# LayerNorm seams of a two-block transformer kernel, by token halves; even_in's banks read by ScalarE

## The chip, the cores and the metric

One core of one Trainium2 chip runs the whole program. The metric is the device time of one execution in microseconds (us). The kernel before took 2296.6 us, the median of three runs (2296.34 to 2301.74).

## The reference

The input is x of 512 tokens by 1024 channels in float32. Two blocks follow one another. The first has a qkv projection, banded attention, an RWKV mixer, gates, an output product and a squared-ReLU feed-forward, with RMS norms. The second has two layers; each is a mixer, a LayerNorm, a convolutional feed-forward and a LayerNorm:

```python
for layer in range(2):
    y = even_mixer(x, ...) if layer % 2 == 0 else odd_mixer(x, ...)
    x = layer_norm(ALPHA * x + y, ln1_g[layer], ln1_b[layer])
    f = conv_ffn(x, ffn_w_up[layer], ffn_conv_w[layer], ffn_conv_b[layer], ffn_w_down[layer])
    x = layer_norm(ALPHA * x + f, ln2_g[layer], ln2_b[layer])

def layer_norm(x, g, b):
    mu = x.mean(-1, keepdims=True)
    var = jnp.square(x - mu).mean(-1, keepdims=True)
    return (x - mu) * lax.rsqrt(var + LN_EPS) * g + b
```

The mean runs over the 1024 channels of a token. Tokens are independent in it. Even_mixer's first product gives 28 tiles of 128 channels with a bias and, for some, a scale.

## The kernel before

**Layout.** Everything is held channel-major: x is 8 tiles (KD = 8) of 128 channels by 512 tokens, `x[:, t, :]`. A dense product computes one output tile (128 by 512, one PSUM bank) as a sum over k. Each k takes three matmuls of 512 columns: high weight part by high input part, high by low, low by high (L321 to L323 in `split_product`). Weights come as a stream of units of eight 128 by 128 blocks. SP loads a unit into one of 3 raw buffers. ACT writes its rounded high part (L169), POOL subtracts that for the low part (L178), into one of 3 split buffers. A split buffer comes free when the last matmul on its unit has run. The classes `Weights`, `Signal` and `Chain` keep the counts; the semaphores of one engine's wait are written out by hand.

**A seam.** Between a stage that ends in a residual and the stage that follows lies a LayerNorm over all channels. There are four: even_out (n_k = 4 blocks per tile) to ffn_up_0, ffn_down_0 (n_k = 22) to odd_in, odd_out (n_k = 8) to ffn_up_1, and ffn_down_1 (n_k = 22) to the last stage, which only norms and stores. `stage_linear` (L1975) computes eight tiles. DVE adds each bank to x (L2073), and to a running sum of x (L2082); ACT squares the tile (L2044) and DVE adds the square to a running sum (L2052). PE waits for no norm there, it only needs banks.

After the eighth tile `layer_norm` (L569) runs, all on 512 tokens. PE turns the three sums into columns of 4 numbers per partition by matmuls of one column (`column_sums`, L434). DVE makes mean and variance in `col` (L595 to L601, 128 by 4), ACT takes the root (L465), DVE the reciprocal (L460), and PE spreads mean and factor over partitions with 8 matmuls of 128 columns (`spread_columns`, L440). Then for each of 8 tiles: DVE adds the negative mean (L607) and scales (L612), in pairs; ACT writes the high part of x plus bias (L589) and x plus bias (L590); POOL subtracts for the low part (L498).

`first_products` (L327) takes the first three tiles of the next stage (AT_FIRST = 3) in step with that. For each of the first six k it waits for the high part, issues two matmuls for each of three tiles (L341, L342), waits for the low part, and issues one for each (L347). So a k gives PE nine matmuls of 512 columns. The last two k of each tile come at the end. All three units of these tiles must be split before.

**The weight queue at a seam.** `Weights.ahead` lets ACT and POOL prepare units up to two beyond those released. In front of the norm's work ACT has one `round_high` and POOL one `subtract_low`, so that three units are ready.

**even_in.** Sixteen jobs (`EVEN_FIRST`) write banks 0 to 3 in turn: twelve tiles and four transposes of tokens (`turn_token`, L937). PE waits before job n for the read of job n - 4. DVE reads each bank (L2196 and L2297), and between two reads does the gates' work for that job number (`gates_dve`, L2238): sums, a scan over tokens, and four calls of `split_rows` (L726, with L731, L732, L734) which writes rows in three bf16 parts. ACT here only rounds weight units and runs `gates_act` at job 5, two pairs of Exp and Ln.

**The last stage.** After each tile's L590, SP stores 256 KB of it to `out_t` (L3096), and waits for all eight.

Of the kernel before, what the change touches and what calls it, by code (L numbers as in the profile page):

```python
# [22 lines left out]
NT = T // P  # L23
D = 1024
# [159 lines left out]
class Before:  # L184

    def __init__(self, pe, act, dve, pool, high, ready, counts, order=tuple(range(KD))):
# [12 lines left out]
def network(nc, x_t, vectors, constants, rel_rev, stream, bias_line, bias_rows, gate_rows, out_t):  # L201
    n_units = stream.shape[0]
    ctx = ExitStack()
    with ctx:
# [93 lines left out]

        side_pe, side_act, side_dve = Signal(sem("side_pe")), Signal(sem("side_act")), Signal(sem("side_dve"))
# [67 lines left out]

        def product(pe, n_tiles, n_k, rhs, read, before=None, beside=None, prior=None, late=None):


            if before is not None:
                before.pe(pe)
                first_products(pe, rhs, before)
                if beside is not None:
                    beside(pe, 1)
# [9 lines left out]
        def weight_programs(block, act=True, before=None):  # L385
# [8 lines left out]
            def _(pool):  # L394
                if before is not None:
                    wts.subtract_low(pool, G, u0 + 1)
                    before.pool(pool)
# [171 lines left out]
        def layer_norm(name, layer, split=True):  # L569

            def pe(p):
                p.wait_ge(norm_dve.sem, norm_dve.at(-1))
                column_sums(p, SUMS, 4, (w[:, SQ_SUM, :],))
                p.wait_ge(norm_dve.sem, norm_dve.at(0))
                column_sums(p, MEAN, 4, (w[:, X_SUM, :],))
                p.wait_ge(norm_act.sem, norm_act.at(0))
                column_sums(p, FACTOR, 4, (w[:, LAST_SQ, :],))
                p.wait_ge(norm_dve.sem, norm_dve.at(1))
                spread_columns(p, SPREAD_MEAN, 0)
                p.wait_ge(norm_dve.sem, norm_dve.at(3))  # L580
                spread_columns(p, FACTOR, 8)

            def act(a):
                root_after_linear(a, LN_EPS, 2)
                for t in range(KD):
                    b = v(name + "_b", KD * layer + t)
                    a.wait_ge(norm_dve.sem, norm_dve.at(t + 4))
                    if split:
                        S.activation(xs[:, 0, t, :], xt(t), ACT.Identity, bias=b).then_inc(norm_high.sem, 1)  # L589
                    S.activation(xt(t), xt(t), ACT.Identity, bias=b).then_inc(norm_act.sem, 1)  # L590

            def dve(d):
                mean, var = col[:, 0:4], col[:, 4:8]
                d.wait_ge(norm_pe.sem, norm_pe.at(2))
                V.tensor_scalar(mean, bank(MEAN, 4, 4), -1.0 / D, None, ALU.mult).then_inc(norm_dve.sem, 1)  # L595
                d.wait_ge(norm_dve.sem, norm_dve.at(1))
                dve_chain.link(d, V.scalar_tensor_tensor(var, bank(MEAN, 4, 4), -1.0 / D, mean, ALU.mult, ALU.mult))
                dve_chain.link(d, V.scalar_tensor_tensor(var, bank(SUMS, 4, 4), 1.0 / D, var, ALU.mult, ALU.subtract))
                d.wait_ge(norm_pe.sem, norm_pe.at(3))
                dve_chain.link(d, V.scalar_tensor_tensor(var, bank(FACTOR, 4, 4), 1.0 / D, var, ALU.mult, ALU.add))  # L600
                V.tensor_scalar(var, var, 0.0, None, ALU.max).then_inc(norm_dve.sem, 1)  # L601
                factor_dve(d, 1)

                def centred(t):
                    if t == 0:
                        d.wait_ge(norm_pe.sem, norm_pe.at(4))
# [2658 lines left out]
```

## Time and profile before

| | |
|---|---|
| runs | 2296.34, 2296.6, 2301.74 us; median 2296.6 us |
| profiled execution | 2297.78 us, span of the profile 2296.0 us, so 1.8 us lie around it |
| PE busy | 2182.6 us, 95% of the span |
| DVE, ACT, POOL busy | 1008.6, 830.9 and 818.6 us |
| mean granted TensorE clock | 0.961 of full speed |

PE runs nearly through. What isn't PE on the chain that ended last is the seams, the chunks of the mixers, and a few waits for DVE. Matmuls of 512 columns last 0.39 us by their rows, and start 0.227 us apart, so a stretch of them is read by starts.

### The profile page before, as it was taken

The page shows a single profiled execution, that of the slowest core. Times are in us where ns is not written, and L with a number is a line of the kernel's source. Part 1 is how long each engine was busy: PE and PEld are TensorE (multiplying, and loading weights), DVE is VectorE, ACT ScalarE, POOL GpSimd, SP SyncE. Part 2 cuts the span into 40 slices and gives each one's busy share as a digit, 9 for nine tenths or more (in the row PEclk, how much of TensorE's full clock was granted, in tenths as well). Part 3 has the DMA queues.
Part 4 walks back from the last instruction along what each step waited for, and adds up shares of the span by engine and source line. Part 5 has one row for each costly group of instructions (what it writes and reads, how often), then busy time and mean ns, then how long its engine had stood idle before and what let it go on. Part 6 is the DMA issues. An engine that isn't in the chain of part 4 may idle for free.

```text
span 2296.0 us, 29683 instructions
## 1 busy us (share of the span) xinstructions
PE 2182.6 (95%) x12396; PEld 1754.9 (76%) x12404; DVE 1008.6 (44%) x1636; ACT 830.9 (36%) x1268; POOL 818.6 (36%) x362
## 2 busy tenths in 40 slices
PE   8999989999899999999997899999999889999997
PEld 6767788888778888776776688888877477888886
DVE  4222855436531121345337644442268465444323
ACT  4345511134342242232335344442243334444322
POOL 4423300034244444442231344444444024444442
PEclk9999988799999999999999899999999989999998
DMA  7222200014223233221111122232312012322331
GB/s 264 92 69 83 74 2 3 2 56 156 74 83 101 92 101 101 83 73 65 47 56 40 53 92 92 96 104 95 101 57 90 19 55 65 102 100 92 101 98 58
DMA packets 53005, 182.97 MB, mean 80 GB/s; under 512 B 5752, under 2 KB 5760, under 8 KB 52744
## 3 DMA queue, kind: packets, MB, share of 16 engines
q1 hardware_dynamic: 52872, 181.08, 23.6%
q8 instruction: 98, 1.61, 0.3%
q14 instruction: 35, 0.29, 0.0%
HBM read 176.32 MB, written 7.62 MB: 80 GB/s over the span
## 4 chain that ended last, share of the span: by engine, by line
PE 87%; DVE 9%; ACT 2%; issue 1%; POOL 1%; DMA 0%; DVEq 0%; SPq 0%; ACTq 0%
PE ps L321 19%; PE ps L323 19%; PE ps L322 19%; PE ps L1506 3%; PE ps L2500 2%; PE ps L341 1%; PE ps L2502 1%; PE ps L347 1%; PE ps L2501 1%; PE ps L342 1%; PE ps L1036 1%; PE ps L3036 1%; PE ps L434 1%; PE ps L1038 1%; PE ps L1037 1%
## 5 line engine op out<-in xcount | busy, mean ns | idle before, releaser
L178 POOL TENSOR_TENSOR split_units<-raw_units,split_units 128x1024 fp32r<-128x1024 f32 x314 | 760.2, 2429 | 1423.2 <-ACT split_units L169 1423.2
L321 PE MATMUL ps<-x_split,split_units 128*128 128x512 f32 x1224 | 482.8, 394 | 8.6 <-POOL split_units L178 6.3
L169 ACT ACTIVATE split_units<-raw_units 128x1024 fp32r<-128x1024 f32 x314 | 329.9, 1052 | 437.9 <-PE ps L323 380.1
L322 PE MATMUL ps<-x_split,split_units 128*128 128x512 f32 x1224 | 478.2, 391 | 0.0
L323 PE MATMUL ps<-x_split,split_units 128*128 128x512 f32 x1224 | 477.9, 390 | 0.0
L321 PEld LDWEIGHTS ps<-x_split,split_units 128*128 128x128 f32 x1224 | 230.9, 189 | 62.8 <-issue 6.5
L322 PEld LDWEIGHTS ps<-x_split,split_units 128*128 128x128 f32 x1224 | 230.9, 189 | 49.2 <-issue 1.7
L323 PEld LDWEIGHTS ps<-x_split,split_units 128*128 128x128 f32 x1224 | 230.9, 189 | 48.6
L321 PE MATMUL ps<-hidden_split,split_units 128*128 128x512 f32 x608 | 237.3, 390 | 0.0
L323 PE MATMUL ps<-hidden_split,split_units 128*128 128x512 f32 x608 | 236.6, 389 | 0.0
L322 PE MATMUL ps<-hidden_split,split_units 128*128 128x512 f32 x608 | 236.5, 389 | 0.0
L2831 DVE SCALAR_TENSOR_TENSOR work<-ps,vec,work 128x511 f32<-128x511 f32 x88 | 66.0, 750 | 225.3 <-ACT work L2820 224.9
L322 PEld LDWEIGHTS ps<-hidden_split,split_units 128*128 128x128 f32 x608 | 114.1, 188 | 24.1 <-issue 0.5
L321 PEld LDWEIGHTS ps<-hidden_split,split_units 128*128 128x128 f32 x608 | 114.1, 188 | 24.0 <-issue 0.5
L323 PEld LDWEIGHTS ps<-hidden_split,split_units 128*128 128x128 f32 x608 | 114.1, 188 | 23.9
L2820 ACT ACTIVATE work<-ps,vec 128x512 f32<-128x512 f32 x88 | 68.6, 780 | 168.0 <-PE ps L323 149.9
L2073 DVE TENSOR_TENSOR x<-x,ps 128x512 f32<-128x512 f32 x29 | 19.9, 687 | 142.0 <-PE ps L323 141.6
L2833 DVE SCALAR_TENSOR_TENSOR work<-ps,vec,work 128x510 f32<-128x510 f32 x88 | 65.9, 749 | 3.1
L2811 ACT ACTIVATE hidden_split<-work 128x512 fp32r<-128x512 f32 x44 | 27.8, 632 | 103.1 <-DVE work L2841 103.1
L1506 PE MATMUL ps<-work 64*64 64x64 f32 x1920 | 64.1, 232 | 0.0
L1506 PEld LDWEIGHTS ps<-work 64*64 64x64 f32 x1920 | 63.6, 148 | 0.1
L341 PE MATMUL ps<-x_split,split_units 128*128 128x512 f32 x120 | 50.8, 423 | 10.6 <-ACT x_split L589 5.0
(434 smaller groups left out, 3283.9 us busy)
## 6 DMA issues: line engine op xcount, KB each, us to landing
raw_units<-stream SPq DMA_DIRECT2D x314, 512.0 KB, 3.4
bias_rows<-bias_line SPq DMA_DIRECT2D x1, 2816.0 KB
gate_rows<-work SPq DMA_DIRECT2D x10, 256.0 KB, 2.1
work<-gate_rows SPq DMA_DIRECT2D x10, 256.0 KB, 2.7
x<-x_t SPq DMA_DIRECT2D x4, 512.0 KB, 6.5
work<-bias_rows SPq DMA_DIRECT2D x1, 2048.0 KB
out_t<-x SPq DMA_DIRECT2D x8, 256.0 KB
vec<-vectors SPq DMA_DIRECT2D x1, 1159.5 KB, 9.2
```

Of the source, the lines that this page charges most:

```text
L169: scalar.activation(self.split[:, u % SPLIT, 0, :], self.raw[:, u % RING, :], ACT.Copy).then_inc(self.high_done, 1)
L178: gpsimd.tensor_tensor(self.split[:, u % SPLIT, 1, :], self.raw[:, u % RING, :], self.split[:, u % SPLIT, 0, :].bitcast(F32), ALU.subtract ...
L321: TE.matmul(out, high, rhs(0, k), start=(k == 0), stop=False)
L322: TE.matmul(out, high, rhs(1, k), start=False, stop=False)
L323: ins = TE.matmul(out, low, rhs(0, k), start=False, stop=last and shift is None)
L341: TE.matmul(bank(m), high, rhs(0, k), start=(i == 0), stop=False)
L1506: ins = TE.matmul(ps[r, out, i * HD:(i + 1) * HD], left(i, r), right(i, r), start=True, stop=True)
L2500: TE.matmul(bank(b % 2), high, a[0], start=(k == 0), stop=False)
L2811: S.activation(hidden2[:, 0, j, :], w[:, y0 + 2 * j % 4, :], ACT.Copy).then_inc(high_out.sem, 1)
L2820: S.activation(w[:, y0 + m % 4, :], bank(m % 4), ACT.Identity, scale=taps(m)[2], bias=v("ffn_b", layer * 44 + (m % 2) * FF2 + m // 2)).the ...
L2831: dve_chain.link(dve, V.scalar_tensor_tensor(y[:, 1:T], b[:, 0:T - 1], taps(m)[1], y[:, 1:T], ALU.mult, ALU.add))
L2833: V.scalar_tensor_tensor(y[:, 2:T], b[:, 0:T - 2], taps(m)[0], y[:, 2:T], ALU.mult, ALU.add).then_inc(tile_read.sem, 1)
```

## The change

It does these things:
- `TH = 256`. The eighth tile of the stage in front of each LayerNorm is computed by `last_by_halves`: all k on tokens 0 to 255 into bank 3, then all k on tokens 256 to 511 into bank 2. In the middle of the first half PE turns the sum of seven squares into columns, at k = 4 of the second half (3 where n_k = 4) it does the column sums of the first 256 tokens, and where n_k = 22 it spreads their mean and factor at k = 13.
- The class `LayerNorm` takes the place of `layer_norm`. Every step exists once for each half. The orders on each engine are written out: DVE does the first three tiles of half 0, then the residual of half 1, two more tiles, the variance of half 1, two more, the reciprocal, the last, then half 1's eight.
- `first_halves` takes the place of `first_products` at these seams. It does tiles 0 and 1 on half 0 for each k, with the column sums of half 1 after k = 3; then the spread of half 1, tile 2 on half 0, and tiles 0, 1, 2 on half 1.
- ACT rounds the first unit of the next stage before the root, the second after it, the third behind tile 4 of half 0. POOL takes the third at tile 5. (In even_out two of them and in odd_out one are still rounded in the stage before.)
- The last stage stores 16 pieces of 128 KB instead of 8 of 256 KB.
- even_in's banks are read by ScalarE. The query scale of 1/8 moves into scale and a scaled bias. The two semaphores on which even_mix waited for DVE's row splits become `ready_out`.

The diff, cut to its core:

```diff
+        def first_halves(pe, rhs, seam):
...
+            def one_block(m, h, k):
+                if k == 0 and h == 0:
+                    pe.wait_ge(wts.low_done, unit + m + 1)
+                high, low = (wts.split[:, (unit + m) % SPLIT, part, k * P:(k + 1) * P] for part in range(2))
+                out = bank(m, h * TH, TH)
+                TE.matmul(out, high, rhs(0, k)[:, tokens(h)], start=(k == 0), stop=False)
+                TE.matmul(out, low, rhs(0, k)[:, tokens(h)], start=False, stop=False)
+                seam.ready(pe, h, k)
+                return TE.matmul(out, high, rhs(1, k)[:, tokens(h)], start=False, stop=(k == UNIT - 1))
+
+            for k in range(UNIT):
+                seam.high(pe, 0, k)
+                for m in range(2):
+                    one_block(m, 0, k)
+                if k == 3:
+                    seam.sums(pe, 1)
+            seam.spread(pe, 1)
+            pe.wait_ge(seam_dve.sem, seam_dve.at(seam.READ_B))
+            for k in range(UNIT):
+                one_block(2, 0, k)
+            for m in range(AT_FIRST):
+                for k in range(UNIT):
+                    seam.high(pe, 1, k)
+                    ins = one_block(m, 1, k)
...
+            def act(self, act):
...
+                wts.round_high(act, S, u0 + 1)
+                root(0)
+                wts.round_high(act, S, u0 + 2)
                 for t in range(KD):
...
+                    tile(0, t)
+                    if t == 2:
+                        self.square(act, 1)
+                    if t == 4:
+                        wts.round_high(act, S, u0 + 3)
+                        root(1)
+                for t in range(KD):
+                    tile(1, t)
...
+                variance(0)
+                factor(0)
+                tiles(0, 0, 3)
+                self.residual(dve, 1)
+                tiles(0, 3, 5)
+                variance(1)
+                tiles(0, 5, 7)
+                factor(1)
+                tiles(0, 7, KD)
+                tiles(1, 0, KD)
...
+                        if h == 0 and t == 5:
+                            wts.subtract_low(pool, G, self.unit + 3)
...
+            def last_by_halves(pe):
...
+                for h in range(2):
+                    b = bank(3 - h, h * TH, TH)
+                    for k in range(n_k):
...
+                        TE.matmul(b, high, src(0, k)[:, tokens(h)], start=(k == 0), stop=False)
+                        TE.matmul(b, high, src(1, k)[:, tokens(h)], start=False, stop=False)
+                        ins = TE.matmul(b, low, src(0, k)[:, tokens(h)], start=False, stop=last and not scaled)
...
+                        if h == 0 and k == n_k // 2:
+                            pe.wait_ge(norm_dve.sem, squares_added(KD - 2))
+                            seam.sums_before(pe)
+                        if h == 1 and k == min(4, n_k - 1):
+                            seam.sums(pe, 0)
+                        if h == 1 and k == 13:
+                            seam.spread(pe, 0)
...
+                def residual(dve, h):
+                    xh = x[:, KD - 1, tokens(h)]
+                    dve.wait_ge(tile_ready.sem, ready_at[h])
+                    V.tensor_tensor(xh, xh, bank(3 - h, h * TH, TH), ALU.add).then_inc(seam_dve.sem, 1)
+                    dve.wait_ge(seam_dve.sem, seam_dve.at(4 * h + seam.READ_A))
+                    V.tensor_tensor(w[:, X_SUM, tokens(h)], w[:, X_SUM, tokens(h)], xh, ALU.add
+                                    ).then_inc(seam_dve.sem, 1)
...
                     if n >= 4:
-                        pe.wait_ge(tile_read.sem, tile_read.at(n - 3))
+                        pe.wait_ge(read_act.sem, read_act.at(n - 3))
...
-                for n, (kind, m) in enumerate(EVEN_FIRST):
-                    dve.wait_ge(tile_ready.sem, tile_ready.at(n + 1))
-                    if kind == "tile":
-                        even_tile(m, n % 4).then_inc(tile_read.sem, 1)
-                    else:
-                        V.tensor_copy(w[:, 40 + m, :], bank(n % 4)).then_inc(tile_read.sem, 1)
+                for n in range(n_jobs):
                     gates_dve(dve, n)
...
                     wts.round_high(act, S, u0 + tiles + SPLIT)
                     gates_act(act, n)
+                    act.wait_ge(tile_ready.sem, tile_ready.at(n + 1))
+                    if kind == "turn":
+                        ins = S.activation(w[:, 40 + m, :], bank(n % 4), ACT.Copy)
...
+                        ins = S.activation(w[:, m, :], bank(n % 4), ACT.Identity, bias=v("ev_b", m))
+                    ins.then_inc(read_act.sem, 1)
```

## Rows read from the trace of the kernel before

**Rows 1.** The page, the chain that ended last, shares by engine.
```profile
PE 87%; DVE 9%; ACT 2%; issue 1%; POOL 1%; DMA 0%; DVEq 0%; SPq 0%; ACTq 0%
```

**Rows 2.** Waits of PE, 985 to 1092 us: us in total, times, longest us.
```profile
PE ps L937 <- DVE work L2297: 5.6, 1, 5.6
```

**Rows 3.** Timeline, end of even_in: start us, us, engine and line; PE, then DVE.
```profile
1032.93 0.66 PE L937 MATMUL ps<-con,work 128*128 128x128 f32 x4
1039.13 1.11 PE L937 MATMUL ps<-con,work 128*128 128x128 f32 x4 [5.55 <-DVE work L2297]
1041.33 0.63 PE L321 MATMUL ps<-x_split,split_units 128*128 128x512 f32 x1
...
1038.39 1.29 DVE L2297 COPY work<-ps 128x512 f32<-128x512 f32 x2
```

**Rows 4.** Windows of 4 us: length, busy PE, PEld, DVE, ACT, POOL, granted clock, DMA.
```profile
1036.00:1040.00 4.00, 0.86 (x5) 0.87 (x5) 3.81 (x9) 0.00 (x0) 0.00 (x0) 0.52 0.41 131
1040.00:1044.00 4.00, 4.00 (x14) 3.17 (x13) 3.66 (x9) 0.00 (x0) 0.00 (x0) 0.62 0.01 2
...
1907.00:1911.00 4.00, 2.08 (x8) 1.78 (x8) 2.70 (x6) 0.76 (x2) 0.00 (x0) 0.50 0.43 131
```

**Rows 5.** Seam behind ffn_down_0, timeline; its last row is the chain's.
```profile
1673.70 0.39 PE L323 MATMUL ps<-hidden_split,split_units 128*128 128x512 f32 x1
...
1682.42 0.72 ACT L589 ACTIVATE x_split<-x,vec 128x512 fp32r<-128x512 f32 x1 [3.15 <-DVE x L612]
...
1683.68 0.73 ACT L589 ACTIVATE x_split<-x,vec 128x512 fp32r<-128x512 f32 x1
1683.84 10.10 POOL L498 TENSOR_TENSOR x_split<-x,x_split 128x512 fp32r<-128x512 f32 x8 [4.93 <-ACT x L590]
...
1700.43 6.96 PE ps L2878 x16
```

**Rows 6.** Ends of the other three seams, timeline: PE, and ACT for the last.
```profile
1299.51 0.39 PE L2007 MATMUL ps<-first_high,mean_weights 128*128 128x512 f32 x1
...
1330.17 0.50 PE L321 MATMUL ps<-x_split,split_units 128*128 128x512 f32 x1 [1.55 <-POOL split_units L178]
...
1901.61 0.39 PE L323 MATMUL ps<-odd_split,split_units 128*128 128x512 f32 x1
...
1932.00 0.50 PE L321 MATMUL ps<-x_split,split_units 128*128 128x512 f32 x1 [1.56 <-POOL split_units L178]
...
2275.55 0.39 PE L323 MATMUL ps<-hidden_split,split_units 128*128 128x512 f32 x1
...
2292.14 1.38 ACT L590 ACTIVATE x<-x,vec 128x512 f32<-128x512 f32 x2 [0.54 <-DVE x L612]
```

**Rows 7.** Groups by line and shape: busy us, mean ns; the last row is timeline.
```profile
L612 DVE SCALAR_TENSOR_TENSOR x<-x,vec,ps 128x512 f32<-128x512 f32 x32 | 23.4, 742 | 2.8 <-PE ps L440 2.8
...
L1655 DVE TENSOR_TENSOR work<-ps,con 128x256 f32<-128x256 f32 x40 | 17.0, 425 | 9.3 <-PE ps L1506 7.9
...
L1118 ACT ACTIVATE work<-work,col 128x256 f32<-128x256 f32 x8 | 4.0, 502 | 2.5 <-DVE col L1069 2.5
...
L169 ACT ACTIVATE split_units<-raw_units 128x1024 fp32r<-128x1024 f32 x314 | 329.9, 1052 | 437.9 <-PE ps L323 380.1 <-PE ps L347 27.5 <-PE ps L792 9.2
...
L178 POOL TENSOR_TENSOR split_units<-raw_units,split_units 128x1024 fp32r<-128x1024 f32 x314 | 760.2, 2429 | 1423.2 <-ACT split_units L169 1423.2
...
1676.95 0.16 DVE L597 SCALAR_TENSOR_TENSOR col<-ps,col 128x4 f32<-128x4 f32 x1
```

**Rows 8.** Timeline of PE: eight matmuls of 128 float32 columns, full 128 by 128 weights.
```profile
158.60 1.04 PE L995 MATMUL ps<-con,work 128*128 128x128 f32 x8
...
1905.39 1.14 PE L440 MATMUL ps<-con,col 128*128 128x128 f32 x8
```

**Rows 9.** DVE's addition of the seventh square in even_out and odd_out, timeline.
```profile
1300.61 0.69 DVE L2052 TENSOR_TENSOR work<-work 128x512 f32<-128x512 f32 x1
...
1898.84 2.05 DVE L2052 TENSOR_TENSOR work<-work 128x512 f32<-128x512 f32 x1
```

More of the change, by code:

```diff
@@ L394, in _ @@
             def _(pool):
+                if before is not None and not before.halves:
+                    wts.subtract_low(pool, G, u0 + 1)
                 if before is not None:
-                    wts.subtract_low(pool, G, u0 + 1)
                     before.pool(pool)
@@ L1993, in squares_added @@
                 return norm_dve.at(dve0 + max(k, 1) + shift)
+            whole = KD if seam is None else KD - 1
+            def last_by_halves(pe):
+                base = wts.block
+                for h in range(2):
+                    b = bank(3 - h, h * TH, TH)
+                    for k in range(n_k):
+                        unit, i = divmod(base + k, UNIT)
+                        if h == 0 and (k == 0 or i == 0):
+                            pe.wait_ge(wts.low_done, unit + 1)
+                        high, low = (wts.split[:, unit % SPLIT, part, i * P:(i + 1) * P] for part in range(2))
+                        last = k == n_k - 1
+                        TE.matmul(b, high, src(0, k)[:, tokens(h)], start=(k == 0), stop=False)
+                        TE.matmul(b, high, src(1, k)[:, tokens(h)], start=False, stop=False)
+                        ins = TE.matmul(b, low, src(0, k)[:, tokens(h)], start=False, stop=last and not scaled)
+                        if h == 1:
+                            wts.block += 1
+                            wts.free(ins, tile_ready if last else None, KD + 1)
+                        if h == 0 and k == n_k // 2:
[5 more added lines that the diff above has]
+                            seam.spread(pe, 0)
+                    if scaled:
+                        ins = TE.matmul(b, mean_weights[:, :], first_high[:, 0, tokens(h)], start=False, stop=True)
+                    ins.then_inc(tile_ready.sem, 1)
@@ new lines, in stage_linear @@
+            if seam is not None:
+                ready_at = [tile_ready.at(KD + h) for h in range(2)]
+                def residual(dve, h):
[5 more added lines that the diff above has]
+                                    ).then_inc(seam_dve.sem, 1)
+                seam.residual = residual
+                seam.unit = (block0 + KD * n_k) // UNIT
@@ L2007, in shift @@
                     return TE.matmul(out, mean_weights[:, :], first_high[:, 0, :], start=False, stop=True)
-                for m in range(0 if before is None else AT_FIRST, KD):
+                for m in range(0 if before is None else AT_FIRST, whole):
                     if m == (2 if before is None else AT_FIRST) and centre:
@@ L2030, in _ @@
                 for m in range(KD):
[L2031 removed]
+                    upto = (block0 + (m + 1) * n_k) // UNIT + SPLIT
+                    if seam is not None and m >= whole - 1:
+                        upto = min(upto, seam.unit)
+                    wts.round_high(act, S, upto)
+                    if m == whole:
+                        act.wait_ge(norm_dve.sem, squares_added(m - 2))
+                        seam.square(act, 0)
+                        continue
                     if m == 0 and scaled:
@@ L3082, in _ @@
                 last.pe(pe)
+                last.sums(pe, 1)
+                last.spread(pe, 1)
             @block.scalar
```

238 lines of the change are left out of this document (162 added, 76 removed).

## The prediction

> **What bounds the kernel now.** The chain of waits on the page comes first: PE holds 87% of it, DVE 9% [rows 1]. So a change pays only where PE stands still, or works at a lower clock. The waits of PE around even_in show one long one, 5.6 us for DVE's read of a bank [rows 2]. The timeline there shows what it costs: four transposes that take 0.66 us elsewhere start at 1039.13 after 5.55 us of nothing and take 1.11 us, and the matmuls behind them last 0.63 us each [rows 3]. The windows say why: the granted clock is at its lower level, 1.2 GHz for 2.4, after the gap [rows 4]. At the seams I read the timelines. Behind ffn_down_0 the last product ends at 1673.70 + 0.39 = 1674.09, and the three tiles that go with the norm end at 1700.43 [rows 5]: 26.3 us, of which their 72 matmuls at 0.227 are 16.3. So 10.0 us of PE are lost there, and as much or more at the others [rows 6]. That is what the change could win. Once the norm runs, PE does nine matmuls per k, 2.04 us, while DVE, ACT and POOL each need 1.26 us per tile: ACT's high parts start 1.26 apart and POOL's eight take 10.10 [rows 5]. PE is covered well there; the loss lies in front of the first tile.
>
> **The prices of half pieces.** PE: the 512-column matmul takes 0.227 us, so half is at least 0.1135 if nothing else binds. Behind each lies a weight load of 128 columns. The nearest row is eight matmuls of 128 float32 columns with full loads: 1.04 us less the 0.27 that one lasts, over seven, is 0.110 each; the same reckoning gives 0.124 in the other row [rows 8]. I take 0.117, ends 0.110 and 0.124. DVE: a 256-column operation with a PSUM operand lasts 0.43 against 0.74 for 512 [rows 7]; a centre and scale pair falls from 1.26 to about 0.72. ACT: 0.72 for 512 [rows 5], 0.50 for 256 [rows 7]; a pair of them from 1.26 to 1.26 - 2 x 0.21 = 0.83. POOL: 10.10 / 8 = 1.26 for 512 and 2.43 for 1024 give about 0.70 for 256. So a whole tile, as two halves, costs ACT 1.66 instead of 1.26: sixteen pieces take 13.3 us instead of 10.1. PE's step per k falls from 2.04 us to 6 x 0.117 = 0.70 in the first part and 0.35 in tile 0's second half. Both lie under ACT's 0.83. **That is the point on which this forecast rests:** the norm starts earlier, but then ACT and POOL set the pace where PE did.
>
> The Trainium skill has a rule against such short matmuls. "TensorE: Matmul & The Clock Gate", Part 3, The mechanism, says that a weight load overlaps matmuls in flight only if it goes to another row group. Rows 8 speak against it here: 0.110 us holds a load and 128 two-pass columns together. By that rule the time would be that of the fourth rival.
>
> **The seam behind ffn_down_0, step by step**, t from the first matmul of its eighth tile. Before: 66 x 0.227 = 15.0, so t = 0 at 1659.1 and the third tile ends at t = 41.4. After:
> - Half 0: 66 x 0.117 and four column sums, 8.2, with the drain 8.4. DVE residual and sum, 2 x 0.43: 9.3. PE goes on with half 1, so its column sums come at 10.0 to 10.5. Variance, five operations of 0.16 [rows 7] with 0.03 between: 11.6.
> - ACT must first round unit u0. Its buffer comes free only at k = 5 of half 1, 10.9, since half 1 uses all weights again; copy 1.05 [rows 7], 12.0; table load and root, 13.5; reciprocal, 13.7; PE's spread, 14.4. DVE's first pair: 15.6, ACT 16.6. POOL meanwhile takes two units' low parts, 2.43 each, until 17.3, so the first low half is there at 18.0. PE ends half 1 at 17.1. **0.9 us of waiting is left of 10.**
> - DVE puts half 1's residual between tiles 2 and 3, from 17.3 to 18.4, so tile 3 leaves DVE at 19.5, ACT at 20.4, POOL at 21.2. PE does k = 3 and then the sums of half 1, 22.2. Variance 23.4. Tile 5 leaves DVE 24.5, ACT 25.5, POOL 26.3, tile 7 at 27.9. PE ends the first part at 28.4: 16 x 3 x 0.117 = 5.6 us of matmuls in 11.4.
> - Spread 29.1. Tile 2's half 31.9, while DVE and ACT begin half 1 at 30.3. ACT's eight pairs of 0.83 end 37.1, POOL 37.9, PE 38.1; tiles 1 and 2, 48 x 0.117 = 5.6: **43.7, which is 2.3 later than before.**
>
> **The other seams**, same steps. odd_out: last tile's start 1902.0 - 24 x 0.227 = 1896.55, next stage's fourth tile 1932.00 [rows 6], 35.4 us. In the first half PE now waits for the sum of seven squares, which DVE ends at 1898.84 + 2.05 [rows 9], a good microsecond sooner once POOL's unit moves behind the norm. The first low part comes at 12.5, part one ends at 22.9, all at 38.4: **+3.0**. even_out: thirteen matmuls before 1299.90 give 1296.95, to 1330.17 [rows 6], 33.2 us. There the wait for the square sum, until 1301.3 [rows 9], now stands in the middle of half 0 with 1.9 us of product behind it. End 38.5: **+5.3**. Both numbers hold that the wait of 1.55 us for the fourth tile's unit [rows 6] goes: tile 0 now ends 6 us before it is due.
>
> Last stage: t = 0 at 2260.95, ACT ends 2293.52 [rows 6], 32.6. After: half 1 at 17.0, its residual 17.5, variance behind tile 4 at 20.3, spread 22.6, then eight pairs at DVE's 0.72: 29.1. PE stands 3.5 us before that spread, so I add 0.5 for it at the lower clock. The last store is half as large, 0.1 less. **-3.1**. SP's sixteen issues come 0.72 apart or more.
>
> even_in: DVE's read goes off PE's path. 5.55 of wait, 0.45 on the transposes, and six matmuls at 0.43 instead of 0.23, 1.2 [rows 2 to 4]: **-7.2**. Cover: ACT's gate work at job 5, four table loads, about 8 us, lies between the reads of jobs 4 and 5, and PE wants read 5 only at job 9, some 20 us on. DVE loses some 7 us of reads and ends its splits before PE reaches even_mix; if not, that gap comes back there. The added scaled bias is 0.2 us on DVE, hidden.
>
> Sum at the full clock: 5.3 + 2.3 + 3.0 - 3.1 - 7.2 = **+0.3 us**. To this comes the clock. At the three split seams PE has long stretches at half load or less, as before the first part, in it (5.6 of 11.4), and beside ACT's 0.83. After such a stretch the old odd_out seam shows 0.50 [rows 4]; from 1911.2 to about 1916.5 its matmuls ran at half speed, a loss of 2.6 us. In the new seams such a fall is partly covered by waits. I take 1.5 us per seam, **+4.5**, ends 0 and 3.3 each.
>
> So 2297.8 + 0.3 + 4.5 = 2302.6 for the profiled execution, whose time was 1.2 above the median; that makes **2301 us**. About 0.3%, 6.9 us, is what a measurement of this kernel can tell from no change.
>
> **Rivals.**
> 1. *The second half's chain hides behind PE.* Then each split seam costs its first wait and PE's own work: ffn_down_0 35.2 instead of 41.4, odd_out 29.0, even_out 29.4, together -16.4; with -3.1 and -7.2 the time is 2270. For it: the old first part never waits once it runs. Against it: 13.3 us of ACT in series with two spreads. Half of that gain gives 2287. Chance of one or the other 0.18.
> 2. *The clock stays low.* If PE is granted half speed through the first part of each seam and again from the spread on, each loses 3 to 5 us: 2308 to 2314. It decides from 2.2 us lost per seam at the lower clock with PE the bound. For it: rows 4, and the low share of matmuls worked out above. Against it: the waits leave slack. Chance 0.33.
> 3. *even_in does not gain*, since the reads queue behind ACT's Exp and Ln or DVE is late for even_mix: 2308. Chance 0.05.
> 4. *Loads don't hide behind 256 columns.* There are 2 x 3 x (22 + 22 + 8 + 4) = 336 halves in last tiles and 3 x 144 = 432 in the first; 768 x 0.1 us is 77: 2378. Rows 8 speak against it. Chance 0.02.
>
> **How the numbers follow.** The forecast, within 0.3%, has 0.42; faster 0.18; rivals 2 to 4 together 0.40. The pace's ends, 0.110 and 0.124, move the sum by 3 us either way, the clock's ends by -4.5 and +5.4. The forecast's own range is 2294 to 2306; to leave out no more than 2 in 10 it goes to 2287 and 2313.
>
> **What the changed profile would show.** Right: starts of the new 256-column matmuls near 0.117 apart; no wait in even_in; PE waiting for POOL's and ACT's halves in tile 0's second half, every 0.83 us, and near k = 5 of the first part; ACT's root 3 to 4 us earlier against half 0's end than the old one against its tile. Wrong, if PE's matmuls in these seams follow without gaps, if their spacing is over 0.15, or if the windows there show 1.00 throughout.

## The result, and the profile after

| | before | after |
|---|---|---|
| median of four runs | 2298.9 us (the three of above and 2301.28) | 2321.45 us (2315.17 to 2324.08) |
| profiled execution, span | 2297.78, 2296.0 us | 2324.08, 2322.2 us |
| PE, DVE, ACT, POOL busy | 2182.6, 1008.6, 830.9, 818.6 us | 2202.4, 1005.4, 853.0, 824.3 us |
| mean granted clock | 0.961 | 0.957 |

The ratio of after to before is 1.0094, with an interval of 1.0068 to 1.0119. The change makes the kernel slower by 22 us. The forecast was 2301 with a range of 2287 to 2313; the measured median lies above all of it.

The page's chain that ended last, by engine, against [rows 1]: PE and DVE have each lost a point, ACT and DMA have each won one.

```profile
PE 86%; DVE 8%; ACT 3%; DMA 1%; issue 1%; POOL 1%; SPq 0%; ACTq 0%; DVEq 0%
```

To see where 26 us of span came from I cut the timelines of PE into stretches that every kernel here has. "even_in" runs from its first matmul (969.19 before) to the first group of four transposes behind it (1088.22), "even_mix" is the part of the mixer from its first matmul on `forget_high` (1206.86 before) to even_out's first matmul, 67 us before. A seam's stretch runs from the start of the eighth tile in front of it to the start of the next such tile; so it holds the seam and what follows it. Behind even_out and odd_out these are products, and they are alike to 0.1 us in all kernels. Behind ffn_down_0 there is the second mixer too, whose time is not steady, so that seam gets a column of its own: from the eighth tile to the end of the next stage's third tile. The last stretch runs to the end of the span. In us, e1 to e12 being the kernels of the experiments:

| kernel | even_in | even_mix | even_out | ffn_down_0 | its seam alone | odd_out | last |
|---|---|---|---|---|---|---|---|
| before | 119.0 | 67.0 | 362.2 | 237.4 | 41.4 | 364.4 | 35.2 |
| **after** | 112.6 | 71.2 | 373.9 | 246.6 | 49.7 | 371.0 | 34.5 |
| e1, even_in only | 111.0 | 67.0 | 362.3 | 237.4 | 41.4 | 364.4 | 35.2 |
| e2, and last | 112.6 | 71.2 | 362.3 | 238.3 | 43.4 | 364.3 | 34.5 |
| e3, e1 and ffn_down_0 | 111.4 | 67.4 | 362.3 | 244.1 | 48.6 | 364.5 | 35.1 |
| e4, e1 and odd_out | 112.6 | 71.2 | 362.3 | 238.3 | 43.4 | 370.8 | 35.1 |
| e5, e1 and even_out | 111.5 | 67.4 | 373.4 | 239.7 | 42.8 | 364.6 | 35.0 |
| e6, order | 111.4 | 67.3 | 369.1 | 241.1 | 45.1 | 367.2 | 35.6 |
| e7, order and unit | 112.6 | 71.2 | 368.9 | 238.4 | 43.4 | 365.9 | 35.7 |
| e8, busy | 112.5 | 71.2 | 374.0 | 243.4 | 47.4 | 371.0 | 34.5 |
| e9, sums moved | 111.0 | 67.1 | 365.0 | 238.2 | 43.1 | 364.7 | 34.2 |
| e10, last's factor | 111.5 | 67.4 | 362.3 | 237.5 | 41.4 | 364.4 | 33.9 |
| e11, whole seams busy | 112.6 | 71.2 | 361.8 | 241.3 | 44.2 | 363.5 | 34.5 |
| e12, e10 and two edits | 111.5 | 67.3 | 362.3 | 237.5 | 41.5 | 364.4 | 35.5 |

After against before: even_in -6.5, even_mix +4.2, even_out +11.7, ffn_down_0 +9.2, odd_out +6.6, last -0.7, and 1.7 in the rest: 26.2. Of ffn_down_0's 9.2 the seam has 8.3 and the mixer behind it 0.8.

Two columns need care. even_in and even_mix move together: of the thirteen changed kernels, those with even_in at 111.0 to 111.5 have even_mix at 67.0 to 67.4, and those with 112.5 or 112.6 have 71.2. And the seam behind ffn_down_0, whole and with the same instructions, took 41.4 to 41.5 us in four traces and 42.8 to 43.4 in three. Windows of e1 (seam 41.4) and e2 (43.4), both from about 24 us after the eighth tile's start (length, busy PE, PEld, DVE, ACT, POOL, granted clock, DMA):

```profile
1676.00:1680.00 4.00, 3.04 (x12) 2.22 (x13) 4.00 (x7) 4.00 (x7) 2.73 (x3) 1.00 0.00 0
```

```profile
1684.00:1688.00 4.00, 3.63 (x9) 2.85 (x10) 4.00 (x8) 4.00 (x8) 2.99 (x3) 0.50 0.00 0
```

The clock came back later in e2. So a difference of 2 us at this seam between two single traces can be the clock's, and not the edit's.

**even_in.** The wait of [rows 3] is gone; eight transposes stand in one row where, after four of them, PE did nothing for 5.55 us. Timeline of PE, after:

```profile
1035.25 1.09 PE L1077 MATMUL ps<-con,work 128*128 128x128 f32 x8
```

**The seam behind ffn_down_0**, which [rows 5] show before. The chain of waits of the kernel after, in order of time (start, us, what), the pieces of PE's plain product left out:

```profile
1681.25 0.79 PE ps L638 x8
1682.60 1.06 ACT split_units L170
1683.68 1.28 ACT L674
1684.97 0.31 ACT col L674
1685.52 1.16 PE ps L651 x8
...
1692.78 0.74 POOL x_split L752
1693.56 0.39 PE ps L389
1694.30 0.80 PE ps L638 x8
1695.90 1.00 DVE col L707
1696.90 0.65 DVE x L718 x2
...
1698.96 0.74 POOL x_split L752
1699.74 0.58 PE ps L389
1703.53 1.72 PE ps L651 x8
1705.27 0.75 DVE x L718 x2
...
1713.82 0.39 PE ps L389
```

Read it downwards. Half 0's sums (L638) lead to ACT's unit (L170), table load and root (L674), and to the spread (L651), as forecast. Then comes a second ring, and it is the costly one: POOL's half of tile 3, PE, the sums of half 1, DVE's variance (L707), and only then DVE's tile 5, ACT, POOL and PE again. DVE's timeline has its own stop there:

```profile
1695.12 0.16 DVE L702 TENSOR_SCALAR col<-ps 128x2 f32<-128x2 f32 x1 [2.98 <-PE ps L638]
```

PE's has the two stops of that ring, and what it runs at around them:

```profile
1670.20 0.28 PE L2149 MATMUL ps<-hidden_split,split_units 128*128 128x256 f32 x1
1670.32 0.28 PE L2150 MATMUL ps<-hidden_split,split_units 128*128 128x256 f32 x1
...
1693.56 0.39 PE L389 MATMUL ps<-x_split,split_units 128*128 128x256 f32 x1 [0.70 <-POOL x_split L752]
...
1695.19 0.42 PE L387 MATMUL ps<-x_split,split_units 128*128 128x256 f32 x1
1695.41 0.42 PE L389 MATMUL ps<-x_split,split_units 128*128 128x256 f32 x1
...
1698.54 0.58 PE L386 MATMUL ps<-x_split,split_units 128*128 128x256 f32 x1 [2.07 <-ACT x_split L681]
...
1701.41 0.41 PE L386 MATMUL ps<-x_split,split_units 128*128 128x256 f32 x1
1701.62 0.41 PE L387 MATMUL ps<-x_split,split_units 128*128 128x256 f32 x1
...
1719.89 3.60 PE L3091 MATMUL ps<-x,vec 128*8 128x512 f32 x8
```

The seam ends at 1719.89, 49.7 us from the first row; before it was 41.4. Half matmuls start 0.120 apart in the first two rows and 0.213 behind the stop of 2.07. The windows (stretch, us, busy PE, PEld, DVE, ACT, POOL, granted clock, DMA) show where the upper level of PE's clock ended:

```profile
1690.00:1694.00 4.00, 3.04 (x21) 2.54 (x21) 2.11 (x6) 2.92 (x8) 2.40 (x4) 1.00 0.42 131
1694.00:1698.00 4.00, 2.47 (x17) 2.17 (x15) 2.74 (x9) 0.76 (x3) 2.67 (x2) 0.64 0.10 13
1698.00:1702.00 4.00, 3.05 (x12) 2.76 (x13) 1.20 (x4) 2.48 (x6) 2.19 (x3) 0.50 0.34 122
```

The clock was lost at about 1695, after PE had stood for 0.26 and 0.70 us and done the column sums, and before the stop of 2.07: the rows at 1695.19 and 1695.41 are already 0.22 apart. In e3, whose seam has the same instructions, matmuls behind these sums still start 0.12 apart and the clock falls in the stop. So the stop isn't what began the fall here.

**The seam behind even_out** has in addition a stop in the middle of half 0. Timeline of PE, then of DVE:

```profile
1296.29 0.28 PE L2149 MATMUL ps<-mlstm_high,split_units 128*128 128x256 f32 x1
...
1300.85 1.05 PE L629 MATMUL ps<-ones,work 128*128 128x1 f32 x8 [3.33 <-DVE work L2247]
...
1311.80 0.58 PE L386 MATMUL ps<-x_split,split_units 128*128 128x256 f32 x1 [1.77 <-ACT x_split L681]
```

```profile
1300.10 0.69 DVE L2247 TENSOR_TENSOR work<-work 128x512 f32<-128x512 f32 x1
1302.59 0.42 DVE L2172 TENSOR_TENSOR x<-x,ps 128x256 f32<-128x256 f32 x1 [1.79 <-PE ps L2163]
```

DVE is free at 1300.79, but reads half 0 only at 1302.59, since PE had stood in half 0 for DVE's square. The first norm matmul comes 15.5 us after the tile's start; with whole tokens it was 14.6. So here the halves start the norm no earlier at all. The clock goes down behind this stop: the windows from 1305 to 1313 show 0.50, half 0's sums last 1.70 us and the spread 2.08, where that spread takes 1.05 at the upper level.

### The profile page after: what moved, and what is told of

Read it like the earlier page. It is cut to its first block, busy times and chain, and to the rows that moved or that the text cites. A ratio compares the mean times of both kernels' runs of the same rounds, so it can differ in the third digit from the quotient of the medians.

```text
span 2322.2 us, 30670 instructions
## 1 busy us (share of the span) xinstructions
PE 2202.4 (95%) x12781; PEld 1785.4 (77%) x12789; DVE 1005.4 (43%) x1717; ACT 853.0 (37%) x1348; POOL 824.3 (35%) x386
## 4 chain that ended last, share of the span: by engine, by line
PE 86%; DVE 8%; ACT 3%; DMA 1%; issue 1%; POOL 1%; SPq 0%; ACTq 0%; DVEq 0%
PE ps L325 19%; PE ps L327 19%; PE ps L326 19%; PE ps L1646 3%; PE ps L2714 2%; PE ps L2716 1%; PE ps L2715 1%; PE ps L1176 1%; DMA raw_units<-stream 1%; PE ps L3248 1%; PE ps L1178 1%; PE ps L1177 1%; DVE work L1773 1%; PE ps L345 1%; PE ps L346 1%
## 5 line engine op out<-in xcount | busy, mean ns | idle before, releaser
L325 PE MATMUL ps<-x_split,split_units 128*128 128x512 f32 x1224 | 483.3, 395 | 5.5 <-POOL split_units L179 3.2
L326 PE MATMUL ps<-x_split,split_units 128*128 128x512 f32 x1224 | 478.6, 391 | 0.0
L327 PE MATMUL ps<-x_split,split_units 128*128 128x512 f32 x1224 | 478.5, 391 | 0.0
L170 ACT ACTIVATE split_units<-raw_units 128x1024 fp32r<-128x1024 f32 x314 | 329.9, 1052 | 377.4 <-PE ps L327 329.7
L325 PE MATMUL ps<-hidden_split,split_units 128*128 128x512 f32 x564 | 220.2, 390 | 0.0
L327 PE MATMUL ps<-hidden_split,split_units 128*128 128x512 f32 x564 | 219.4, 389 | 0.0
L326 PE MATMUL ps<-hidden_split,split_units 128*128 128x512 f32 x564 | 219.4, 389 | 0.0
L326 PEld LDWEIGHTS ps<-hidden_split,split_units 128*128 128x128 f32 x564 | 105.9, 188 | 22.4 <-issue 0.5
L325 PEld LDWEIGHTS ps<-hidden_split,split_units 128*128 128x128 f32 x564 | 105.9, 188 | 22.3 <-issue 0.5
L327 PEld LDWEIGHTS ps<-hidden_split,split_units 128*128 128x128 f32 x564 | 105.9, 188 | 22.1
L2247 DVE TENSOR_TENSOR work<-work 128x512 f32<-128x512 f32 x36 | 50.8, 1410 | 13.0 <-ACT work L2239 12.1
```

The costliest lines, as they stand in the source:

```text
L170: scalar.activation(self.split[:, u % SPLIT, 0, :], self.raw[:, u % RING, :], ACT.Copy).then_inc(self.high_done, 1)
L325: TE.matmul(out, high, rhs(0, k), start=(k == 0), stop=False)
L326: TE.matmul(out, high, rhs(1, k), start=False, stop=False)
L327: ins = TE.matmul(out, low, rhs(0, k), start=False, stop=last and shift is None)
L2247: V.tensor_tensor(w[:, SQ_SUM, :], a, w[:, SQ + k % 2, :], ALU.add).then_inc(norm_dve.sem, 1)
```

## The experiments

**One part at a time (e1 to e5).** The kernel has both norms in it and a list of the seams that take the one by halves: none in e1, ffn_down_1 in e2, ffn_down_0 in e3, odd_out in e4, even_out in e5. The kernel before was run beside each group of experiments (medians 2300.11 for e1 to e4, 2301.03 for e5 to e8, 2300.75 for e9 to e11, 2297.87 for e12), and the ratios are to that median; between groups the ratios are to be compared, not the times.

```diff
-        ln1 = [LayerNorm("ln1", layer) for layer in range(2)]
+        split_seams = ()
+        ln1 = [norm_of("even_out", "ln1", 0), norm_of("odd_out", "ln1", 1)]
```

> Only the part in even_in: ScalarE reads its banks; all four LayerNorm seams are whole, as in the kernel before. Theory A (the trace after is typical): even_in's wait goes, PE is 5.2 us ahead up to 1220 us, but even_mix gives about 4 us of it back in stretches at the lower clock, so 2296 to 2299 us. Theory B (those low stretches of even_mix were a chance of that one execution): the full gain stays, 2291 to 2294 us.

Measured 2295.57 us against 2300.11, ratio 0.998 (0.9969 to 0.999). The profiled run, at 2291.17 us the fastest of its eleven, keeps the whole gain: even_in 8.1 us shorter, even_mix as before. The median gains only 4.5 us and lies between the two theories. So the loss in even_mix isn't in every execution of the change; whether the change makes it more frequent isn't shown, since the kernel before has one trace only. Of 14 traces, 8 have even_mix at 67.0 to 67.4 and 6 at 71.2, and up to there the changed kernels are alike. The 4 us are in stretches where PE is half idle in both, and the clock falls in one and not in the other. Windows of after, then of before:

```profile
1228.00:1232.00 4.00, 1.88 (x8) 1.16 (x7) 3.86 (x11) 2.65 (x4) 0.00 (x0) 0.86 0.00 0
1252.00:1256.00 4.00, 2.33 (x10) 1.60 (x11) 3.47 (x10) 3.23 (x4) 0.02 (x1) 0.85 0.00 0
```

```profile
1232.00:1236.00 4.00, 1.87 (x9) 1.17 (x9) 3.83 (x12) 2.54 (x4) 0.00 (x0) 1.00 0.00 0
1252.00:1256.00 4.00, 2.11 (x9) 1.38 (x8) 3.86 (x8) 1.88 (x3) 0.00 (x0) 1.00 0.00 0
```

> The part in even_in and the seam into the last stage by halves; the other three seams whole. Theory A (what the trace after shows of this seam, first matmul of the eighth tile to ACT's last: about the same as before): within 1 us of the kernel with even_in's part alone. Theory B (my forecast): 3.1 us below it.

2293.83 us, 0.9976 (0.9967 to 0.9985). In the table the seam gains 0.7, the median 1.7 against e1, within the intervals of both. Theory A is nearer; my 3.1 isn't there.

> The part in even_in and the seam behind ffn_down_0 by halves; the other three whole. Theory A (the loss is made inside the seam: the chain runs 2 us late, DVE waits for the second half's sums between two tiles, and the clock falls to its lower level): 8 us above the kernel with even_in's part alone, the seam 49 to 50 us from the first matmul of the eighth tile to the end of the third tile, where the kernel before has 41.4. Theory B (the forecast with its own clock term): 3.8 us above. Theory C (the seams only hurt together, through the weight stream): within 1 us.

2299.28 us, 0.9998 (0.9989 to 1.0007), so 3.7 above e1. The table says +6.7 (244.1 for 237.4), and +7.2 for the seam by itself, 48.6 us. The median is nearer to B, the trace to A; C falls. A whole seam that takes 43.4 in some of e1's executions would bring the two nearer; that is argued, not shown.

> The part in even_in and the seam behind odd_out by halves; the other three whole. Theory A (loss made inside the seam): 7 us above the kernel with even_in's part alone, the seam 42 us against 35.4 before. Theory B (the forecast): 4.5 us above. Theory C (only together): within 1 us.

2301.59 us, 1.0007 (0.9997 to 1.0017), 6.0 above e1; the stretch +6.4. Theory A.

> The part in even_in and the seam behind even_out by halves; the other three whole. Theory A (the trace after: from the start of even_out's eighth tile to that of ffn_down_0 11.7 us longer): 12 us above the kernel with even_in's part alone, 2307 to 2308. Theory B (the forecast, 5.3 for the steps and 1.5 for the clock): 7 us above, 2302. Theory C (what is left when the other parts' medians are taken off the full change, 21.4 + 4.5 + 1.7 - 3.7 - 6.0): 18 us above, 2313.

2306.17 us, 1.0027 (1.0015 to 1.0038), 10.6 above e1; the stretch +11.1, with 2.3 more in the one behind it (1.3 in the whole seam and 0.9 in the mixer, neither of them edited). Theory A, and C falls. Added as ratios the five parts make -0.20, -0.04, +0.18, +0.27 and +0.47%, together +0.68%, the lower end of the interval of the full change. The stretches add up to within 1 us. That the ratios leave 0.26%, some 6 us, over may be the two forms of even_in and even_mix and chance, with four runs of the full change; it isn't settled.

**The ring in the norm (e6, e7).** In e6 half 1's variance, root and reciprocal go behind half 0's last tile:

```diff
-                tiles(0, 3, 5)
-                variance(1)
-                tiles(0, 5, 7)
-                factor(1)
-                tiles(0, 7, KD)
+                tiles(0, 3, KD)
+                variance(1)
+                factor(1)
```

and ACT's `root(1)` behind its tile 7.

> The full change, with the second half's variance, root and reciprocal moved on DVE and ACT from between the first half's tiles 4, 5 and 7 to behind tile 7. Theory A (what the forecast missed is that DVE, standing between two tiles for sums that wait for PE, stops the first half's last tiles, and the clock falls in that stop): PE's wait of 2.1 us at the sixth k goes, each split seam ends 2 to 5 us earlier, the whole 8 to 15 us below the full change. Theory B (the clock falls because each k is only half a load): the seams lose as much, within 3 us of the full change. Theory C (the order was right, a later variance puts the second half's chain back): 3 to 6 us slower than the full change.

2307.81 us, 1.0036 (1.0022 to 1.005): 0.58% or 13 us below the full change. Theory A. The stretches fall by 4.8, 5.5 (4.6 in the seam) and 3.8; only the last one, where no product waits, grows by 1.1. In the timeline of PE the wait of 2.07 for ACT at the sixth k is gone: behind the sums (second row) it stops only at that k's low part, 1.48 (third row). The clock stays at 1.00 in that seam, though PE's rows up to these sums come as in the full change. So e6 has two things at once, the order and the clock, which e8 tells apart.

```profile
1685.14 0.39 PE L389 MATMUL ps<-x_split,split_units 128*128 128x256 f32 x1 [0.71 <-POOL x_split L750]
1685.73 0.94 PE L638 MATMUL ps<-ones,work 128*128 128x1 f32 x8
1689.21 0.39 PE L389 MATMUL ps<-x_split,split_units 128*128 128x256 f32 x1 [1.48 <-POOL x_split L750]
```

The row of 1.48 is POOL's: its unit of 2.37 us stands in front of tiles 5 to 7. In e7 it goes behind them:

```diff
-                        if h == 0 and t == 5:
+                        if h == 1 and t == 0:
                             wts.subtract_low(pool, G, self.unit + 3)
```

> As the kernel before it, and the next weight unit's rounding on ACT and its low part on POOL (2.4 us) moved behind the first half's tile 7 too. Theory A: POOL no longer stands in front of tiles 5 to 7, a further 1 to 3 us per split seam, the whole 13 to 22 us below the full change. Theory B (POOL's unit was hidden): the same as the kernel with the order alone.

2303.83 us, 1.0014 (1.0002 to 1.0026), by the ratio a further 5 us; the two intervals overlap. By stretches 2.7 at ffn_down_0, of which 1.7 in the seam, 1.3 at odd_out, 0.2 at even_out: theory A at two seams, and not at even_out. A second effect shows on DVE. Timelines of e6, DVE and POOL, and of e7, DVE:

```profile
1687.49 1.01 DVE L707 TENSOR_SCALAR col<-col 128x2 f32<-128x2 f32 x1
```

```profile
1686.11 2.37 POOL L179 TENSOR_TENSOR split_units<-raw_units,split_units 128x1024 fp32r<-128x1024 f32 x1 [0.21 <-ACT split_units L170]
```

```profile
1690.39 0.17 DVE L706 TENSOR_SCALAR col<-col 128x2 f32<-128x2 f32 x1
```

The smallest instruction of the chain, 128 by 2 from SBUF to SBUF, ended at 1688.50, with POOL's 1688.48, and lasted 1.01 for 0.17. The four before it read PSUM and lasted 0.16. In the full change the same instruction lasted 1.00 and is on the chain (1695.90 above), so this is a part of the ring's cost. The Trainium skill has this in "GPSIMD Engine Reference", 8. Key points: GpSimd shares its SBUF interfaces with VectorE, whose instructions collide with it in a two-port mode or with two SBUF inputs. The trace agrees that there are such collisions; this instruction has one SBUF input, and whether it ran in the two-port mode no run shows.

**The clock (e8).** The full change, with matmuls on PE that nobody reads:

```diff
+            busy(20)
             for k in range(UNIT):
+                if k == 5:
+                    busy(12)
                 seam.high(pe, 0, k)
```

> The full change, with matmuls whose result nobody reads added on PE ahead of the first half's first tile (20 of 256 columns, 2.4 us at 0.12) and ahead of its sixth k (12, 1.4 us), at the three split seams; they write a bank that is free there. Theory A (the fall of the clock is a large part of the seams' loss): the windows of the seams show 1.00 instead of 0.5 to 0.7, and 2 to 4 us per seam come back, 6 to 12 us below the full change. Theory B (the waits set the end, the clock costs nothing beside them): within 2 us, whatever the clock shows. Theory C (the added matmuls delay more than the clock gives back): 3 to 8 us slower.

2317.64 us, 1.0068 (1.0056 to 1.008), 0.26% or 6 us better by the ratio, but the intervals overlap (1.0068 to 1.0119 for the full change), and the traces show less than that. Windows of that kernel where the full change had 0.64 and 0.50:

```profile
1691.00:1695.00 4.00, 3.73 (x32) 3.53 (x31) 2.35 (x9) 0.75 (x3) 2.56 (x2) 1.00 0.07 9
1695.00:1699.00 4.00, 2.87 (x20) 2.60 (x21) 1.09 (x4) 2.37 (x6) 2.21 (x3) 1.00 0.31 122
```

ffn_down_0's stretch falls by 3.2 with that, of which the seam has 2.2 and the mixer behind it, which the edit doesn't touch, 0.9. The sixth k still starts 28.3 us after the eighth tile, as in the full change, and the gain lies behind it: the first part ends at 31.7 instead of 33.1, and the spread lasts 1.05 instead of 1.91. even_out's and odd_out's stretches don't move, though the clock rose there too (at even_out 0.92 for 0.50, 16 us into the stretch). At even_out the sixth k starts at 24.8 in both kernels: there the ring set the end. Theory A for one seam, B for two. The added matmuls stand behind half 0's sums and spread. What the lower clock costs in those, at even_out, can be read from e5 alone: there the spread ran near the upper level, 1.16 us for 2.08, and the stretch is 0.5 us shorter.

**even_out's half 0 (e9).** Both orders of e7, for the seams in front of a product; the last stage keeps its own. And:

```diff
-                        if h == 0 and k == n_k // 2:
-                            pe.wait_ge(norm_dve.sem, squares_added(KD - 2))
-                            seam.sums_before(pe)
                         if h == 1 and k == min(4, n_k - 1):
+                            pe.wait_ge(norm_dve.sem, squares_added(KD - 2))
+                            seam.sums_before(pe)
                             seam.sums(pe, 0)
```

with a wait for the seventh tile's read ahead of half 1, which takes its bank.

> As the kernel with order and unit moved (that order now only at the three split seams in front of a product; the last stage has the change's own order), and PE's column sums of the first seven squares moved from the middle of half 0 to just ahead of half 0's own sums, so that half 0's product does not stand behind DVE's seventh square. Theory A (at even_out the stop of 3.3 us in half 0 is on the chain): there half 0 is read about 1.7 us earlier, the seam 38 to 39 us instead of 40.2; with 1.2 us won back in the last stage the whole is 2 to 4 us below that kernel, 2300 to 2302. Theory B (at even_out DVE, with three 512-column operations per tile, is the bound and PE's stop only fills its time): the seam stays at 40 us, 2302 to 2303.

2296.01 us, 0.998 (0.997 to 0.9989), by the ratio 8 us below e7, of which the last stage's own order has 1.5. Theory A, with more than it said: even_out's stretch falls by 3.9. DVE reads half 0 as soon as its square is added, 4.55 us from the tile's start (1292.05) for 6.30:

```profile
1295.87 0.69 DVE L2253 TENSOR_TENSOR work<-work 128x512 f32<-128x512 f32 x1
1296.60 0.42 DVE L2178 TENSOR_TENSOR x<-x,ps 128x256 f32<-128x256 f32 x1
```

and the first norm matmul comes after 11.7 us instead of 15.5. So three moves of an order, with not one piece of work less, take the full change from 1.0094 to 0.998. Its seams in front of products are then at +2.8, +1.7 (43.1 for 41.4, but within what whole ones took) and +0.3 against whole ones: nearly all of the loss is gone, and there is no gain.

**The last seam (e10, e12) and whole seams (e11).** e10 is e2 with one move:

```diff
-                tiles(0, 5, 7)
+                tiles(0, 5, 6)
                 factor(1)
-                tiles(0, 7, KD)
+                tiles(0, 6, KD)
```

> The kernel with even_in's part and the last seam by halves, with DVE's reciprocal of the second half moved from behind the first half's tile 6 to behind tile 5. Theory A (the reciprocal is ready for 1 us before DVE comes to it, and PE's spread waits): the end comes 0.5 to 0.7 us earlier, eighth tile to end 33.9 instead of 34.5. Theory B (DVE's work sets the end, whatever its order): within 0.2 us.

2290.14 us, 0.9958 (0.9944 to 0.9972): **the fastest kernel of the study** by its median of five runs, faster than before and after. The stretch is 33.9 for 34.5. Theory A. Against e2 the median is 0.18% lower, 4 us; the move explains 0.6 of it by the trace, and the two intervals overlap.

> The kernel with even_in's part and the last seam by halves, and in the three whole seams matmuls whose result nobody reads on PE (128 columns, 4 ahead of each of the first two waits, 8 between the two spreads, 14 behind the second). Theory A (the clock's fall in the whole seams costs what the lower-clock spreads and sums take longer, and at odd_out 2.6 us of product): the windows there show 1.00, the seams get 1 to 3 us shorter each, the whole 3 to 7 us below the same kernel without them, 2287 to 2291. Theory B (PE waits for DVE and ACT there, and their chain does not care): within 1.5 us. Theory C (the added matmuls stand in front of sums and spreads that are due): 1 to 3 us slower.

2293.35 us, 0.9969 (0.9957 to 0.998), with e2 at 0.9976: no difference that these runs can tell. Behind that are -0.5 at even_out, -0.8 at odd_out and +3.0 at ffn_down_0 against e2. But of these 3.0 the seam has 0.9, and 2.2 lie in the mixer behind, which is not edited. For the whole kernel B is nearest. At ffn_down_0 PE was busy all the time, with matmuls of 1 and 128 columns, and the clock fell nonetheless:

```profile
1674.00:1675.00 1.00, 1.00 (x11) 1.00 (x11) 0.49 (x3) 0.39 (x1) 1.00 (x1) 1.00 0.00 0
1676.00:1677.00 1.00, 1.00 (x7) 1.00 (x6) 0.55 (x2) 0.00 (x0) 0.00 (x0) 0.50 0.37 86
```

> The fastest kernel so far (even_in's part, the last seam by halves, the reciprocal behind tile 5) with two more edits in that seam: the sums of the first seven squares moved to just ahead of half 0's own, and 16 matmuls of 128 columns whose result nobody reads ahead of the last spread, which lasts 2.07 us at the lower clock and 1.05 at the upper. Theory A (that spread is on the chain of the end, and work in front of it keeps the clock up): eighth tile to end 32.6 to 32.9 instead of 33.9, the whole about 1 us lower, 2289. Theory B (the added matmuls run at the lower clock themselves and end after the reciprocal): 33.6 to 34.5, no gain or a small loss.

2294.31 us, 0.9984 (0.9973 to 0.9994), and the stretch 35.5: theory B, a loss of 1.6 against e10. By the ratios the loss is 0.26%, 6 us, and the intervals don't overlap; the trace accounts for 1.6 of that, and the rest isn't explained. Two edits are in it at once. Each added float32 matmul shows as two records, so 16 of them ran for 5.45 us, more than I had counted, and the spread that waited for nothing but them came at 2280.11:

```profile
2274.83 5.45 PE L3361 MATMUL ps<-con 128*128 128x128 f32 x32
2280.11 1.06 PE L651 MATMUL ps<-con,col 128*128 128x128 f32 x8
```

The spread did run at the upper level, 1.06 for 2.07. With fewer of them it might pay; that wasn't tried.

## Why the prediction was wrong

In its own order, with t from the first matmul of ffn_down_0's eighth tile:

- **Half matmuls at 0.117.** Measured 0.120 in every seam at the upper clock, 0.213 at the lower. 276 of them at this seam make 0.8 us. Right, though one of the two rows it came from was misread: the spread of [rows 8] (1905.39) is four matmuls, each in two records, and not eight. The Trainium skill's rule of "TensorE: Matmul & The Clock Gate", Part 3, that a weight load overlaps only matmuls of another row group, isn't borne out: by it I had 2378. The matmuls of 512 columns, 0.227 apart with a load behind each, spoke against it before, so the fourth rival had no case of its own for 256.
- **Half 0's chain.** Sums 10.5, root 13.5, spread 14.4 were forecast; measured are 11.8, 15.1, 16.5. PE's four sums take 0.8 to 1.05, and each hand-over between engines some tenths. 2 us late here; at odd_out the first low part came at 13.7 for 12.5.
- **The step that failed** is the next: "Variance 23.4. Tile 5 leaves DVE 24.5, ACT 25.5, POOL 26.3, tile 7 at 27.9. PE ends the first part at 28.4." I let the variance of half 1 pass through DVE in 1.2 us with the tiles flowing on. It is a ring through PE, DVE, ACT and POOL. DVE stood 2.98 us in it, tile 5 left ACT at 28.7 and not at 25.5, POOL put its unit into the hole, and PE ended the first part at 33.1, 4.7 late. With the clock kept up (e8) it ended at 31.7, with the order undone (e6) at 29.4, with the unit moved too (e7) at 27.7: the clock has 1.4 of it, the ring the rest. Undoing that order and that unit gives back 18 us of 22 by the ratios and 17.6 by the two spans, with the clock's part in it.
- **even_out, +5.3.** I saw the wait in half 0 and priced it "with 1.9 us of product behind it". It stood in front of DVE's read of half 0, not beside it, and the clock fell behind it. Measured +11.7; order and unit take back 5.0 (e6, e7) and the moved sums 3.9 (e9).
- **The clock, +4.5.** Its fall was there (0.64, 0.50). At ffn_down_0 it began before the long stop, and what began it isn't shown; with the order changed (e6, e7, e9) it wasn't seen there. Kept up, it gives 2.2 us at one seam, where I had 1.5, and nothing at two. Rival 2 has the sign, and seams that lost 4.9, 4.5 and 2.1 beyond the forecast look like its 3 to 5 us each, but most of that was another mechanism: the likeness is luck.
- **The last seam, -3.1.** -0.7. I counted eight pairs from the spread's issue at 22.6. Measured: issue at 23.7, 2.08 us of spread at the lower clock, and only then DVE's first pair. A pair at 0.72 was right.
- **even_in, -7.2.** -8.1 in e1's trace and -6.5 in the profiled run: right for the stretch. The median of e1 shows 4.5 (its interval 2 to 7). That a mixer further on gives 4.2 back in some executions, by the clock, I had not thought of.
- **The signs.** The new matmuls are 0.120 apart, even_in has no wait, and in tile 0's second half PE waits for POOL every 0.80 us, as listed under "Right". So these signs came true in a kernel that missed the range, and didn't test the step that failed.
- **The first rival** (the second half's chain hides, 2270 to 2287) isn't reached even by e9, whose split seams cost nearly what whole ones do and gain nothing. Its 2287 was wrongly worked out: half of the 16.4 us, with the other two parts whole, gives 2278. Against it stands that sixteen half pieces at ACT's 0.80 are 12.8 us in series where eight whole ones take 10.1 [rows 5].

So of the 21.5 us between the sum of 2302.6 and the measured 2324.1, even_out has 4.9, ffn_down_0 5.4 (4.5 in the seam, 0.8 in the mixer behind it), odd_out 2.1, the last seam 2.4, even_in with even_mix 4.9, and the rest 1.7.

## What to carry to other kernels

When a chain is cut in two so that its halves can overlap, draw both chains on each engine's queue and look where the second's reduction sits: an engine that waits there for its own earlier output, through three others, stops the first half's tail too. Put such a step behind the last piece that doesn't depend on it, and put optional work (a weight unit) where the queue is idle, not in front of the chain. In this kernel halves paid where nothing but the chain remains (the last stage, 0.7 to 1.3 us by the traces), and not in front of a product that a whole piece already keeps busy. And read a second trace of the same code before a difference of some us between two single traces is put down to an edit.

## What was not expected of the hardware

- The same instructions of even_mix ran in two ways, 67.0 to 67.4 us in 8 traces and 71.2 in 6, with granted clocks of 1.00 or 0.85 over like stretches of half-idle PE, and the whole seam behind ffn_down_0 took 41.4 or 42.8 to 43.4. Such 2 to 4 us can hide or feign an effect when single profiles are compared.
- The granted clock fell to 0.50 in a stretch in which PE was busy throughout with matmuls of 1 and 128 columns (e11), and stayed at 1.00 with the same edit at even_out.
- A DVE instruction of 128 by 2 elements from SBUF to SBUF lasted 1.01 us for 0.17, until POOL's operation beside it ended.
